# Raw products of a norm's input ahead of the norm, in the second layer, and a transposed start: one change to a two-block transformer kernel

## The reference

```
mod = silu(c) @ w_ada + b_ada              # 12 column blocks; shifts sh, scales sc, gates g
hx  = rmsnorm(x, g_pre_mix) * (1 + sc1) + sh1
q, k, v, u, gv, f = split(hx @ w_in)       # q, k rotated by position
attn, sgu, four = attention(q, k, v, ck, cv), gating(u, gv), fourier(f)
y   = concat(rmsnorm each of the three) * g_mix @ w_out
x   = x + g1 * rmsnorm(y, g_post_mix)
hx2 = rmsnorm(x, g_pre_ff) * (1 + sc2) + sh2
x   = x + g2 * rmsnorm(relu(hx2 @ w_ff1)**2 @ w_ff2, g_post_ff)
```

## Time and profile before

| | us |
|---|---|
| median of 3 runs | 2374.93 (2369.65 to 2376.91) |
| the profiled execution | 2370.18 |
| its span | 2368.4 |
| PE busy | 2277.5 (96%) |
| DVE / ACT / POOL busy | 810.9 / 489.8 / 145.8 |

### The profile page before, as it was taken

One profiled execution on the slowest core, in us unless ns is written; L12 is line 12 of the kernel. 1 busy time (PEld: TensorE's weight loads), 2 busy tenths in 40 slices (PEclk: granted clock), 3 DMA queues, 4 the chain that ended last, 5 costly groups with the idle time before them and its releaser, 6 DMA issues.

```text
span 2368.4 us, 34248 instructions
## 1 busy us (share of the span) xinstructions
PE 2277.5 (96%) x14400; PEld 1669.0 (70%) x14400; DVE 810.9 (34%) x2062; ACT 489.8 (21%) x1153; POOL 145.8 (6%) x150
## 2 busy tenths in 40 slices
PE   6999999999999999999999989999999999999998
PEld 4777888888877678887689845655555555556556
DVE  2245554577434420004665322222222222222224
ACT  3255410000023432002543211111111111111113
POOL 1000211144200000000000000000000000000000
PEclk9999999999999999999999999999999999999999
DMA  8722222133234343444323757999999999999993
GB/s 366 279 107 107 107 80 99 72 142 142 107 142 146 139 178 143 164 156 173 142 107 142 292 231 301 426 427 426 427 425 427 426 427 426 427 427 427 426 427 125
DMA packets 42261, 601.61 MB, mean 254 GB/s; under 512 B 4688, under 2 KB 5328, under 8 KB 5744
## 3 DMA queue, kind: packets, MB, share of 16 engines
q1 hardware_dynamic: 41616, 593.30, 61.7%
q10 hardware_dynamic: 480, 5.97, 0.6%
HBM read 598.20 MB, written 1.05 MB: 253 GB/s over the span
## 4 chain that ended last, share of the span: by engine, by line
PE 84%; DMA 10%; DVE 2%; ACT 2%; issue 1%; POOL 0%; SPq 0%; POOLq 0%; DVEq 0%; PEldq 0%; ACTq 0%
PE PS L1112 16%; PE PS L1136 8%; PE PS L866 8%; PE PS L641 7%; PE PS L676 6%; PE PS L625 6%; PE PS L728 5%; PE PS L516 4%; PE PS L615 3%; DMA BIG<-in_w_up 3%; DMA RG<-in_w_up 3%; PE PS L714 2%; PE PS L1041 2%; PE PS L1148 2%; DMA SM<-in_w_down 2%; DMA RG<-in_w_ada 1%
## 5 line engine op out<-in xcount | busy, mean ns | idle before, releaser
L2412 DVE TENSOR_SCALAR STAT<-PS 128x128 f32<-128x128 f32 (+1 forms) x128 | 37.9, 296 | 669.0 <-PE PS L1112 669.0
L1112 PE MATMUL PS<-BIG,XS 128*64 128x256 f32 (+1 forms) x2016 | 239.1, 388 | 3.9 <-DMA BIG<-in_w_up 3.9
L1112 PEld LDWEIGHTS PS<-BIG,XS 128*64 128x64 f32 (+1 forms) x2016 | 146.7, 139 | 94.3 <-issue 21.1
L1291 ACT ACTIVATE BIG<-PS 128x256 f32<-128x256 f32 (+2 forms) x205 | 85.4, 430 | 480.4 <-PE PS L641 138.9
L1112 PE MATMUL PS<-RG,XS 128*64 128x256 f32 (+1 forms) x1520 | 178.5, 385 | 4.9 <-DMA RG<-in_w_up 4.9
L866 PE MATMUL PS<-XS,RG 128*128 128x256 f32 x768 | 172.1, 382 | 5.0 <-DVE XS L1868 4.1
L866 PEld LDWEIGHTS PS<-XS,RG 128*128 128x128 f32 x768 | 145.7, 192 | 26.6 <-issue 6.9
L1112 PEld LDWEIGHTS PS<-RG,XS 128*64 128x64 f32 (+1 forms) x1520 | 108.3, 138 | 73.4 <-issue 15.7
L1717 ACT ACTIVATE STAT<-STAT 128x128 f32<-128x128 f32 (+1 forms) x128 | 40.1, 313 | 574.5 <-DVE STAT L2412 574.5
L1834 DVE TENSOR_SCALAR HOLD<-PS 128x256 f32<-128x256 f32 x27 | 11.4, 423 | 393.8 <-PE PS L492 299.8
L625 PE MATMUL PS<-HN,RG 128*128 128x256 f32 x640 | 140.5, 382 | 4.0 <-ACT HN L1338 4.0
(11 more groups left out here) (353 smaller groups left out, 3281.2 us busy)
## 6 DMA issues: line engine op xcount, KB each, us to landing
BIG<-in_w_up SPq DMA_DIRECT2D x64, 2048.0 KB, 27.3
RG<-in_w_up SPq DMA_DIRECT2D x48, 2048.0 KB, 27.8
RG<-in_w_ff SPq DMA_DIRECT2D x32, 2048.0 KB, 7.8
BIG<-in_w_down SPq DMA_DIRECT2D x32, 2048.0 KB, 28.7
RG<-in_w_ada SPq DMA_DIRECT2D x24, 2048.0 KB, 7.8
RG<-in_w_down SPq DMA_DIRECT2D x24, 2048.0 KB, 28.6
RG<-in_w_in SPq DMA_DIRECT2D x23, 2048.0 KB, 8.0
SM<-in_w_up SPq DMA_DIRECT2D x16, 2048.0 KB, 27.5
```

What stands on the lines that cost most here:

```text
L1112: i = pe.matmul(half_of(b, h, sides), Xg[:, k, 0:cap], w[:, k, h * wd:h * wd + wd], start=False, stop=k == 7)
L1291: i = act.activation(dst, banks[b][rows, part], fn)
```

## The change

Five edits; all the rest of the program stays as it is.

1. Start. The input is stored as two halves. SP loads C's half ahead of the weights, and X's behind the first `w_in` block. PE takes C's mean first, transposes each modulation block behind its product, and does the first four `w_in` tiles of C in two halves (`w_in_halves`: k 0 to 3 of the four tiles, then k 4 to 7), with the second modulation block's transposition behind the first of these groups. X's mean moves into them. DVE and ACT follow this order.
2. Second layer, into `w_in`. The four q tiles are made from `XQ = XS * gain`, not yet divided by the root, with the shift as a 257th column (`w_in_early`, two tiles at a time). DVE multiplies the result by the root (`early_q`, into `QE_`), ACT adds the 257th column. X's mean becomes a summed one and stands between them; the two `ada` blocks move behind the fifth and sixth tile. The rotations come later.
3. `w_out` of the second layer: the first four of the eight products (Fourier and gating) of tiles 0 to 2 are done before the attention's mean, of tile 3 behind it (`w_out_half`).
4. Second layer, into `ff1`: as in 2 for the first four hidden tiles (`ff1_early`, `scaled_x`, `hidden_early`), and X's mean becomes a summed one between them. Its first weight block goes to a slot of its own (8), in the softmax's space.
5. Semaphores for these.

```diff
@@ start: PE @@
-            ada(0, 3)
             mean_summed(("mix", 0, C), range(8), own(HN, C), ones)
             ada_turn(0, 2)
+            ada(0, 3)
             ada_turn(0, 3)
-            mean_summed(("mix", 0, X), range(8), own(HN, X), ones)
             ada(0, 0)
+            ada_turn(0, 0)
             ada(0, 1)
-            ada_turn(0, 0)
-            ada_turn(0, 1)
-            for i in range(12):
+            w_in_halves(range(4))
+            for i in range(4, 12):
                 w_in(0, C, i)
@@ w_in_halves @@
+                for half in range(2):
+                    for i in tiles:
+                        b = F.at["in", 0, C, i][0] if half else take(("in", 0, C, i))
+                        for k in range(4 * half, 4 * half + 4):
+                            if i == 0:
+                                pe.wait_ge(s_hn, NORM["mix", 0, C] + k + 1)
+                            m = pe.matmul(banks[b][:, 0:256], w[:, k, 128 * i:128 * i + 128], own(HN, C)[:, k, :],
+                                          start=k == 0, stop=k == 7)
+                        if half:
+                            m.then_inc(s_full[b], 1)
+                        elif i == 0:
+                            ada_turn(0, 1)
+                        if half and i == 1:
+                            mean_summed(("mix", 0, X), range(8), own(HN, X), ones)
@@ start: SP; ACT's own load of XS goes @@
             sp.dma_start(SM1[:, 0:first], A["sm1"][:, 0:first]).then_inc(s_cc, 16)
+            sp.dma_start(own(XS, C), A["xs"][:, C]).then_inc(s_in[C], 16)
...
+                if key == ("w_in", 0, C, 0):
+                    sp.dma_start(own(XS, X), A["xs"][:, X]).then_inc(s_in[X], 16)
@@ second layer, into w_in: PE @@
             down_plain()
-            ada(1, 4)
+            w_in_early((0, 1))
+            mean_summed(("mix", 1, X), range(8), own(HN, X), ones)
             mean_post("ff", 0, C)
-            mean(("mix", 1, X), range(8), own(HN, X), ones)
-            ada(1, 5)
-            ada_turn(1, 4)
-            for i in range(12):
+            w_in_early((2, 3))
+            for i in range(4, 12):
                 w_in(1, X, i)
-                if i == 0:
-                    ada_turn(1, 5)
-                if 1 <= i <= 5:
-                    rotate(1, i - 1)
-                if i == 3:
+                if 4 <= i <= 5:
+                    ada(1, i)
+                if 5 <= i <= 6:
+                    ada_turn(1, i - 1)
+                    rotate(1, 2 * i - 10)
+                    rotate(1, 2 * i - 9)
+                if i == 6:
                     mean_summed(("mix", 1, C), range(8), own(HN, C), ones)
-                if i == 5:
+                if i == 7:
+                    rotate(1, 4)
+                if i == 8:
                     w_in(1, C, 4)
                     w_in(1, C, 5)
@@ w_in_early; ff1_early is the same with XN, w_ff1 and s_xn @@
+                for k in range(8):
+                    if tiles[0] == 0:
+                        pe.wait_ge(s_xq, 8 + k + 1)
+                    for n in tiles:
+                        m = pe.matmul(banks[b[n - tiles[0]]][:, 0:257], w[:, k, 128 * n:128 * n + 128], XQ[k],
+                                      start=k == 0, stop=k == 7)
@@ second layer, w_out and into ff1: PE @@
+                if i == 8:
+                    w_out_half(1, X, 0, 0)
+            w_out_half(1, X, 1, 0)
+            w_out_half(1, X, 2, 0)
             merge("mA", 1, X)
-            for n in range(8):
+            w_out_half(1, X, 3, 0)
+            for n in range(4):
+                w_out_half(1, X, n, 1)
+            for n in range(4, 8):
                 w_out(1, X, n)
             mean_post("mix", 1, X)
             ada(1, 10)
             ada(1, 11)
             ada_turn(1, 10)
-            mean(("ff", 1, X), range(8), own(HN, X), ones)
+            ff1_early((0, 1))
             ada_turn(1, 11)
-            for c in range(8):
+            ff1_early((2,))
+            mean_summed(("ff", 1, X), range(8), own(HN, X), ones)
+            ff1_early((3,))
+            for c in range(1, 8):
                 for n in range(4):
                     ff1(1, X, c, n)
@@ ACT: scaled_q; scaled_x is the same with XN; both take the place of squares @@
+                for k in range(8):
+                    act.wait_ge(s_x, POST["ff", 0, X] + (k + 1))
+                    act.activation(XQ[k][:, 0:256], own(XS, X)[:, k, :], ACT.Copy, scale=coef(1, 0)[:, k, 0:1]).then_inc(s_xq, 1)
+                    act.activation(own(HN, X)[:, k, :], own(XS, X)[:, k, :], ACT.Square).then_inc(s_sq, 1)
@@ DVE: early_q after prenorm; the same into HE in front of ff1 @@
+                dve.tensor_tensor(QE_[:, n, :], banks[b][:, 0:257], STAT[:, 0:257], ALU.mult).then_inc(s_free[b], 1)
@@ POOL @@
+            pool.wait_ge(s_x, POST["ff", 0, X] + 8)
+            sums(("mix", 1, X), range(8))
             sums(("mix", 1, C), range(8))
...
+            pool.wait_ge(s_x, POST["mix", 1, X] + 8)
+            sums(("ff", 1, X), range(8))
```

More of the change, by code:

```diff
@@ L96, in __init__ @@
     def __init__(self):
-        self.order, self.slot, self.nth, self.count, self.end, self.now, self.before = [], {}, {}, [0] * 8, {}, {}, {}
+        self.order, self.slot, self.nth, self.count, self.end, self.now, self.before = [], {}, {}, [0] * 9, {}, {}, {}
     def get(self, key, slot):
@@ L434, in chunk @@
                 new = key not in R.slot
-                if new:
+                if new and key == ("w_ff1", 1, 0):
+                    slot = 8
+                    R.before[key], R.end[key], R.end["softmax"] = "softmax", through, ("o", 1, X, 7)
+                elif new:
                     ended = list(F.at)
@@ L1455, in _ @@
             row(0, 3)
-            root(("mix", 0, X), X)
             row(0, 0)
-            row(0, 1)
             shifted("mix", 0, C)
+            squares(0, X, "mix")
             for i in range(12):
@@ L1581, in _ @@
             row(1, 10)
-            squares(1, X, "ff")
+            scaled_x()
             row(1, 11)
@@ L1585, in _ @@
             shifted("ff", 1, X)
-            for k in range(32):
+            for k in range(4):
+                hidden_early(k)
+            for k in range(4, 32):
                 hidden(1, X, k)
@@ L2187, in _ @@
             turned(1, 10)
+            D.up(dve.memset(STAT[:, 256:257], 1.0))
             prenorm("ff", 1, X)
+            dve.wait_ge(s_dve, D.n)
+            for k in range(4):
+                b = full(("h", 1, X, k))
+                dve.tensor_tensor(HE[:, k, :], banks[b][:, 0:257], STAT[:, 0:257], ALU.mult).then_inc(s_free[b], 1)
             turned(1, 11)
```

146 lines of the change are left out of this document (112 added, 34 removed).

## The result

| | before | after |
|---|---|---|
| median of 4 runs, us | 2372.29 (2367.93 to 2376.91) | 2345.47 (2342.57 to 2347.67) |
| ratio to before, 95% interval | | 0.9881 (0.9859 to 0.9903) |
| profiled execution / its span | 2370.18 / 2368.4 | 2347.01 / 2345.1 |

The change gained 26.8 us by the medians and 23.3 by the two spans. Forecast were 22.4 and 2352. The direction was right; the time is 6.5 us under the forecast and 0.5 under the low end of the forecast range. The median of before is lower than in the table ahead of the prediction because a fourth run is in it.

What follows compares the result with a forecast made beforehand. PE, busy 96% of the span, bounds the kernel. Gains 4.3 + 6.1 + 2.8 + 9.25 = 22.4 us take the profiled 2370.18 to 2347.8, or 2352.5 from the median; forecast 2352, range 2346 to 2361.

Steps and rivals of the forecast that it cites:

- Into the second layer: First layer to second: fewer mean matmuls and two waits removed, less a new 0.5 wait; gain 6.1 us, from 3 to 6.6.
- `w_out`: Second layer's w_out: products done ahead remove the 2.78 us wait for POOL; gain 2.8 us.
- into `ff1`: Second layer into ff1: fifth hidden tile at 854.3, not 863.55; gain 9.25 us, allowed 7 to 9.5.
- rival of lost margins: Second layer: POOL's or ACT's chain 2 us late at three places, clock falls before ff1; 2360 us, chance 0.09.
- Start: Program start: PE begins w_in at 31.0 when its weights land, five tiles end at 50.6, not 54.91; gain 4.3 us.
- rivals of slow 1 KB runs: Start: input halves in 1 KB runs load slower than bytes say, start gains 0 or loses; 2357 us, chance 0.12.
- slower case: Start: at 0.25 us a run each half takes 16 us, 21 lost against 18.1 won elsewhere; 2378 us, chance 0.03.
- second rival: Second layer's margins, 0.5 to 1.7 us wide on denser ACT and DVE programs, do not hold; 2360 us, chance 0.09.
- savings were not hidden: Rival: weights stream from 1300 us on; if its own loads set its start, nothing is left; 2375 us, chance 0.04.
- the step that the clock falls only behind a gap of about 3 us: Start: a 3.0 us gap ahead of w_in may halve PE's clock, costing 1.7 us; half was taken.
- The rest of the program only moves: Expert phase: its loads wait for earlier work's signals, so they come as much sooner; gain there 0.
- The median: The profile lies 4.75 us under the median of the runs, so the sum from the median gives 2352.5.

Runs made afterwards that it cites:

- start_only: The kernel before with only the change's start edit: 2368.94 us, ratio 0.9984 to before.
- after_again: The changed kernel, unedited, timed and profiled a second time: 2347.61 us, ratio 0.9887 to before.
- warm: The changed kernel with 12 idle matmuls in PE's gaps of the start: 2348.53 us, ratio 0.9907 to before.
- both: The changed kernel with fifteen idle matmuls in the start's gaps and seven around the router: 2342.04 us, ratio 0.9870 to before.
- after_third: The changed kernel, unedited, timed and profiled a third time: 2348.26 us, ratio 0.9885 to before.
- pad6: The changed kernel with six one-column matmuls, result unread, in PE's idle time at the start: 2353.76 us, ratio 0.9927 to before.
- pad18: The changed kernel with eighteen one-column matmuls, result unread, in PE's idle time at the start: 2348.07 us, ratio 0.9904 to before.
- before_pad10: The kernel before with ten one-column matmuls, result unread, in PE's idle time at the start: 2367.6 us, ratio 0.9977 to before.
- hold: The changed kernel with ten idle matmuls in PE's waits around the router and first gather: 2349.41 us, ratio 0.9908 to before.

## Why the prediction was right or wrong

**Into the second layer, `w_out`, into `ff1`: right.** 6.1, 2.8 and 9.25 were forecast; 6.3, 2.5 and 8.9 came, and 6.1, 2.5 and 8.9 when each was done alone. The steps held one by one: mean done at 692.0 (692.7 forecast), C's mean not late, wait in front of the fifth tile 0.47 (0.45 forecast), clock 1.00. The rival of lost margins falls.

**Start: the mechanism right, one size given to what varies.** "Gain 4.3, from 3.5 to 5.2" held in `start_only`, 4.0 at the end of the first layer, and failed in after's profile, 0.5. Over the profiles without idle matmuls in the start, the first layer ends at 682.9 to 685.6 us with before's start (six) and at 680.3 to 685.2 with the changed one (five). The means are 1.7 us apart.

The loads behaved nearly as said: C's half landed by 6.99 us, where ACT's squares begin, and `w_in` began at 31.55, released by its own weights. While X's half moved the queue ran at 369 GB/s (30 to 34 us), against 418 and 428 in the windows behind: some 0.5 us by estimate from these rates. So the rivals of slow 1 KB runs fall, and with them the slower case; the second rival's margins held, and the savings were not hidden. By the table of the Trainium skill (DMA: Bandwidth & Descriptors, "Measured") it would have been 34.7; that table is for loads issued by GpSimd, and for these queued ones the measurement decides against it.

Two things were missing. First, the step that the clock falls only behind a gap of about 3 us ("between the 2.70 that left the clock alone and the 3.51 that did not"): it fell behind 1.54 us and stayed low for 10 us in after, for 3.5 in `after_again` and `start_only`. The sum had 0.85 for it; the tiles show 2.9 in after, by `warm` (21.7 against 18.8 us). The length of a gap alone does not tell: 1.57 us in before left the clock at 1.00. Short waits of 0.6 to 0.8 stood ahead of after's fall, but before had one of 1.29 ahead of its 1.57, so what decides stays open. "HAM oscillation" in the Trainium skill (TensorE: Matmul & The Clock Gate) warned that a wait for DMA between matmul groups can bring a fresh fall; the trace agrees that it can, behind waits much shorter than those of the section's example (the two gaps that the prediction set beside it were waits for ACT).

Second, what is late after 53 us. The gain, 1.67 at 53.24, was 0.2 at 76.28, since PE stood 1.57 us for a modulation block that came at 76.3, where before's came at 76.5:

```profile
76.28 1.92 PE L474 MATMUL PS<-RG,SM 128*32 128x512 f32 x16 [1.57 <-DMA RG<-in_w_ada]
```

I had checked `w_in`'s second block and none further on. How much is left depends on the execution: this block starts at 73.1 us in `after_again`, 73.5 in `warm`, 73.0 in `both`, 76.4 in `after_third`. Why it lands 3 us apart is open. The part's worth in time is 2.6 us by the medians alone on before (ratio 0.9984), and 2.5 us taken off after.

**"The rest of the program only moves": wrong, by 5.3 us.** The work and its loads did move as they are, up to the first gather to 0.1 us. But the change took 12 matmuls out of PE's program. With them went a wait of 2.84 us at a jump (2.9) and the slow clock behind it (3.0), and a wait of 2.0 came a step later (2.7 the other way). The other 2.1 us are a fall of the clock in the first step that does not follow the count (1.7), and the rest (0.4). `pad6`, `pad18` and `before_pad10` show the wait's part with the work unchanged: about 0.4 us for each instruction between 16699 and 16711, 5.9 down to 1.1. Against `before_pad10`, which is rid of the wait too, after's gain is 2367.6 - 2348.3 = 19.3 us and `both`'s 25.6. So 5.4 us, by medians, could have been had without the change.

**The median.** I carried over that before's profiled execution lay 4.75 us under its median. After's lies 1.54 over its own. That is 6.3 us, nearly all of the 6.5 missed: one execution's distance from the median of three says little where the runs of these two kernels lie 5 to 15 us apart. With the fourth run before's median was 2372.29, only 2.1 over its profile. In the profiles my terms were 3.8 too much at the start and 5.3 too little at the end, so that 22.4 came close to 23.3 by luck.

## What to carry to other kernels

Where a stream of loads sets the pace at the end of a program, find the last event that still delays it: before that point each microsecond counts once, behind it none (892.2 to 892.9 us in sixteen profiles of thirteen programs). A gain that appears in code that the change does not touch wants a control with idle instructions: six or ten one-column matmuls moved this kernel by +6 and by -5 us. When loads in front of a change come sooner, follow the queue until the gain is used, not only to the next wait. And read a stretch in several profiles of one program before giving it one number: this start ended its layer at times 5 us apart in five profiles.

## What was not expected of the hardware

- TensorE's wait at a jump into code not yet run hangs on how many instructions lie ahead: 5.5 to 5.9 us at 16699, 3.4 at 16703, 2.8 to 3.1 at 16705, 1.1 at 16711, 0.4 to 0.5 at 16715, none at 16693. Profiles of one count agree within 0.5 us, whatever the work, and each wait ends 2.1 to 2.2 us after a 16 KB transfer of the instruction queue.
- The clock fell behind a gap of 1.54 us (after, 27 us), where 1.57 (before, 25 us) left it alone, and in `hold` near 1336, in a stretch with no idle time but with narrow products; in another execution of one program it returned at 30 us in place of 37.
- A load of 1 MB in runs of 1 KB costs little in the queue: C's half was in use at 6.99 us, and with X's half in it the queue ran at 369 GB/s for 4 us, where it runs at 418 to 451 otherwise.
